# RMS norm statistics by short columns: squares added on VectorE, root and reciprocal on 128x4, spread by four matmuls

## The reference

```python
def rms_norm(t, w):
    tf = t.astype(jnp.float32)
    y = tf * lax.rsqrt(jnp.mean(tf * tf, axis=-1, keepdims=True) + NORM_EPS)
    return (y * w.astype(jnp.float32)).astype(t.dtype)

def modulate(h, shift, scale):
    return h * (1.0 + scale[:, None, :]) + shift[:, None, :]
...
        h = modulate(rms_norm(x, mix_norm[layer]), sh1, sc1)
...
        x = x + g1[:, None, :] * y
        h = modulate(rms_norm(x, ffn_norm[layer]), sh2, sc2)
        x = x + g2[:, None, :] * swiglu(h, ffn_w1[layer], ffn_w2[layer])
```

## Time and profile before

| | us |
|---|---|
| median of three runs | 4071.24 |
| the runs | 4070.95, 4071.24, 4079.08 |
| span of the profiled execution | 4077.1 |
| TensorE busy | 3536.0 |
| VectorE busy | 1910.2 |
| ScalarE busy | 1105.3 |

### The profile page before, as it was taken

One profiled execution on the slowest core, in us unless ns is written; L12 is line 12 of the kernel. 1 busy time (PEld: TensorE's weight loads), 2 busy tenths in 40 slices (PEclk: granted clock), 3 DMA queues, 4 the chain that ended last, 5 costly groups with the idle time before them and its releaser, 6 DMA issues. The chain is left out here.

```text
span 4077.1 us, 35826 instructions
## 1 busy us (share of the span) xinstructions
PE 3536.0 (87%) x12594; PEld 2393.3 (59%) x12594; DVE 1910.2 (47%) x2585; ACT 1105.3 (27%) x1425; POOL 77.1 (2%) x148
## 2 busy tenths in 40 slices
PE   4997889999789998858999963999979679989987
PEld 1444468877458787523888521588847347558433
DVE  5756266536358824243664498366333433143001
ACT  1221243233432214211442101244242322132000
POOL 0000000000000000000000000000000000000000
PEclk9897999999899999868999986999989889999988
DMA  5331146522035532101333210233323112222111
GB/s 211 96 123 53 42 153 192 188 83 73 16 119 196 172 99 79 52 0 52 93 97 96 69 47 11 73 98 95 96 81 100 36 48 86 82 63 97 52 62 62
DMA packets 100408, 360.85 MB, mean 89 GB/s; under 512 B 11152, under 2 KB 11169, under 8 KB 100065
## 3 DMA queue, kind: packets, MB, share of 16 engines
q1 hardware_dynamic: 77936, 276.07, 21.1%
q0 software_dynamic: 20080, 75.27, 5.7%
q10 hardware_dynamic: 2304, 8.39, 0.5%
HBM read 357.59 MB, written 2.10 MB: 88 GB/s over the span
## 5 line engine op out<-in xcount | busy, mean ns | idle before, releaser
L1583 DVE TENSOR_TENSOR weight_lo<-weight_ring,weight_hi 128x1024 fp32r<-128x1024 f32 (+1 forms) x390 | 468.7, 1204 | 931.5 <-ACT weight_hi L1104 927.5
L1104 ACT ACTIVATE weight_hi<-weight_ring 128x1024 fp32r<-128x1024 f32 (+1 forms) x390 | 406.9, 1045 | 1266.0 <-PE proj_banks L683 926.3
L683 PE MATMUL proj_banks<-h_hi,weight_hi 128*128 128x512 f32 x1584 | 617.2, 390 | 9.6 <-DVE weight_lo L1583 9.6
L683 PE MATMUL proj_banks<-h_lo,weight_hi 128*128 128x512 f32 x1584 | 617.0, 389 | 0.0
L683 PE MATMUL proj_banks<-h_hi,weight_lo 128*128 128x512 f32 x1584 | 616.9, 389 | 0.0
L640 PE MATMUL proj_banks<-h_tiles,weight_ring 128*128 128x512 f32 x768 | 348.2, 616 | 62.1 <-DVE scratch L1591 38.3
L1617 DVE RECIPROCAL scratch<-scratch 128x512 f32<-128x512 f32 (+1 forms) x39 | 129.2, 3312 | 479.9 <-ACT scratch L1104 479.9
L683 PEld LDWEIGHTS proj_banks<-h_hi,weight_hi 128*128 128x128 f32 x1584 | 297.8, 188 | 73.5 <-issue 11.6
L683 PEld LDWEIGHTS proj_banks<-h_lo,weight_hi 128*128 128x128 f32 x1584 | 297.6, 188 | 61.9
L683 PEld LDWEIGHTS proj_banks<-h_hi,weight_lo 128*128 128x128 f32 x1584 | 297.8, 188 | 61.5
L640 PE MATMUL proj_banks<-scratch,weight_ring 128*128 128x512 f32 x640 | 294.9, 624 | 27.0 <-DMA weight_ring<-in_w_dnr 27.0
(11 more groups left out here) (256 smaller groups left out, 4277.8 us busy)
## 6 DMA issues: line engine op xcount, KB each, us to landing
weight_ring<-in_w_up SPq DMA_DIRECT2D x176, 512.0 KB, 3.6
ada_ring<-in_ada POOLq DMA_DIRECT2D x96, 512.0 KB, 3.8
weight_ring<-in_w_dn SPq DMA_DIRECT2D x64, 512.0 KB, 3.5
weight_ring<-in_w_br SPq DMA_DIRECT2D x32, 512.0 KB, 3.6
weight_ring<-in_w_upr SPq DMA_DIRECT2D x32, 512.0 KB, 3.5
weight_ring<-in_w_dnr SPq DMA_DIRECT2D x32, 512.0 KB, 4.4
scratch<-in_ada POOLq DMA_DIRECT2D x24, 512.0 KB, 4.6
weight_ring<-in_w_dn SPq DMA_DIRECT2D x32, 384.0 KB, 3.1
```

Source lines behind the costliest of these rows:

```text
L683: last = mm(proj.banks[:, u % RING, :], stationary(split0 + n)[:, w], moving(k), start=k + m == 0, stop=k == kt - 1 and m == 2)
L1104: return nc.scalar.activation(out, in_, func, **kw)
L1583: return v.tensor_tensor(out, a, b, op)
```

## The change

In words, for each of the eleven norms:

- **Sum.** TensorE no longer multiplies eight squared tiles of 512 columns by ones. VectorE adds squares 1 to 6 to square 0 (`sum_up`). TensorE then takes 128 tokens of the total as the stationary operand and one column of ones as the moving one, four times, and again four times with square 7. The sums stand in four columns of PSUM, tokens on partitions.
- **Where the adds stand.** For norms 1 to 8 in the residual loop: ahead of the residual of tile k, from k = 2 on, the square of k-1 is added. For norms 0, 9 and 10 all six stand at the head of VectorE's norm.
- **Root and reciprocal** are taken of 128x4. A root of one constant column is put after square 6.
- **Spread.** Four matmuls, with column j of the reciprocal read as a 128x128 stationary operand (step 0) and the identity as the moving one, write 128x512 to a second bank ("bc", r), and the multiply reads it from PSUM. TensorE waits for the reciprocal there.
- **Weight chunks.** ScalarE's two roundings move from ahead of square 7 to behind it, ahead of the root. VectorE's two splits move from ahead of the reciprocal to behind it, ahead of the wait for the spread.
- **Modulated and split.** ScalarE makes h_hi from H(k) with gain and shift in one pass; H(k) itself is modulated by VectorE, in place, ahead of each subtraction. In plain split norms VectorE now waits for each multiply.
- **dn0 to dn3.** `round_down` is gone; ScalarE rounds the chunks among the squares.

```diff
-    k = [("ss", 0)]
+    k = [("ss", 0), ("bc", 0)]
...
+PLAIN_SPLIT = (4, 5, 7)
+STD, INV = 160, 164
...
     def norm(r):
-        sum_squares(("ss", r), lambda k: (s["sq_ready"], 8 * r + k + 1), lambda k: T(squares_at(r) + k), KD)
+
+        bank = open_bank(mix, ("ss", r))
+        for half, (sem, n) in enumerate(((s["sq_summed"], 6 * (r + 1)), (s["sq_ready"], 8 * (r + 1)))):
+            pe.wait_ge(sem, n)
+            for j in range(NB):
+                squares = T(squares_at(r) + (KD - 1 if half else 0))
+                last = mm(bank[:, j:j + 1], squares[:, j * P:(j + 1) * P], c.square("ones")[:, 0:1], start=half + j == 0, stop=half + j == NB,
+                          skip_group_check=True)
+        last.then_inc(mix.full_sem, 1)
+        bank = open_bank(mix, ("bc", r))
+        pe.wait_ge(s["rstd_ready"], r + 1)
+        for j in range(NB):
+            last = mm(bank[:, j * P:(j + 1) * P], c.small[:, INV + j:INV + j + 1].broadcast_to([P, P]), c.square("ident"), start=True, stop=True)
+        last.then_inc(mix.full_sem, 1)
...
-    def round_down(layer):
-
-        for n in range(SPLIT_RING, 3 * KD):
-            round_chunk(f"dn{layer}", n)
...
             elif r in NORM_AFTER:
-                act.wait_ge(*proj.emptied((NORM_AFTER[r], k)))
+                stage = NORM_AFTER[r]
+                if stage in SPLIT:
+                    for n in range(max(3 * k + 2, SPLIT_RING), min(3 * k + 5, 3 * KD)):
+                        round_chunk(stage, n)
+                act.wait_ge(*proj.emptied((stage, k)))
...
-            if r in SPLIT_UP and k == KD - 2:
-
-                up = SPLIT_UP[r]
-                for n in range(SPLIT_RING):
-                    round_chunk(up, n)
-        root(("ss", r), T(RSTD), D)
+            if k == KD - 2:
+
+                st.link(f(c.small[:, STD:STD + 1], eps, ACT.Sqrt))
+        if r in SPLIT_UP:
+
+            for n in range(SPLIT_RING):
+                round_chunk(SPLIT_UP[r], n)
+        act.wait_ge(*mix.filled(("ss", r)))
+        ins = f(c.small[:, STD:STD + NB], mix.bank(("ss", r))[:, 0:NB], ACT.Sqrt, scale=1.0 / D, bias=eps)
+        ins.then_inc(mix.emptied(("ss", r))[0], 1)
...
-                ins = f(H(k), H(k), ACT.Identity, scale=c.g(use, k), bias=c.m(layer, part, k))
-                ins.then_inc(s["h_raw"] if r in SPLIT_NORMS else s["h_ready"], 1)
                 if r in SPLIT_NORMS:
-                    round_h(r, k)
+                    st.done(f(c.norm_hi(r, k), H(k), ACT.Identity, scale=c.g(use, k), bias=c.m(layer, part, k)), s["h_rounded"])
+                else:
+                    f(H(k), H(k), ACT.Identity, scale=c.g(use, k), bias=c.m(layer, part, k)).then_inc(s["h_ready"], 1)
...
+    def sum_up(r, k):
+
+        total = T(squares_at(r))
+        dve.wait_ge(s["sq_ready"], 8 * r + k + 1)
+        st.done(tt(total, total, T(squares_at(r) + k), ALU.add), s["sq_summed"])
+
     def norm(r):
+        if r not in NORM_AFTER:
+            for k in range(1, KD - 1):
+                sum_up(r, k)
+        dve.wait_ge(*mix.emptied(("ss", r)))
+        st.done(v.reciprocal(small[:, INV:INV + NB], small[:, STD:STD + NB]), s["rstd_ready"])
         if r in SPLIT_UP:
             for n in range(SPLIT_RING):
                 rest_chunk(SPLIT_UP[r], n)
-        inverse(("ss", r), T(RSTD))
+        dve.wait_ge(*mix.filled(("bc", r)))
+        rstd = mix.bank(("bc", r))
...
-                st.done(tt(H(k), X(k), T(RSTD), ALU.mult), s["xn_ready"])
+                ins = tt(H(k), X(k), rstd, ALU.mult)
+                st.done(ins, s["xn_ready"])
...
-                ins = stt(out, X(k), c.v(name, at + k), T(RSTD), ALU.mult, ALU.mult)
+                ins = stt(out, X(k), c.v(name, at + k), rstd, ALU.mult, ALU.mult)
...
+        dve.sem_inc(*mix_release(mix, ("bc", r)))
         if r in SPLIT_NORMS:
             for k in range(KD):
+                if r in MODULATED:
+                    use, layer, part, _ = MODULATED[r]
+                    dve.wait_ge(s["h_rounded"], 8 * SPLIT_NORMS.index(r) + k + 1)
+                    st.link(ts(H(k), H(k), c.g(use, k), ALU.mult, c.m(layer, part, k), ALU.add))
...
     def residual(stage, gate=None, bias=None):
 
+        after = [r for r in NORM_AFTER if NORM_AFTER[r] == stage][0]
         for k in range(KD):
...
+            if k >= 2:
+                sum_up(after, k - 1)
             dve.wait_ge(*proj.filled(key))
```

More of the change, by code:

```diff
@@ L228, in mixing_keys @@
         k += [("av", *units[n - 2])] if n >= 2 else []
-    k += [("ss", 1), ("ss", 2)]
+    k += [("ss", 1), ("bc", 1), ("ss", 2), ("bc", 2)]
     k += [("stat_s", t) for t in range(8)] + [("pool", g) for g in range(4)]
@@ L234, in mixing_keys @@
         k += [("sb", h - 2)] if h >= 2 else []
-    k += [("ss", 3), ("ss", 4)]
+    k += [("ss", 3), ("bc", 3), ("ss", 4), ("bc", 4)]
     k += [("acol", 0)]
@@ L241, in mixing_keys @@
         k += [("mn", h, 0), ("mn", h, 1), ("md", h), ("stat_m", h)]
-    k += [("ss", 5), ("ss", 6), ("lnm", 0), ("lnv", 0), ("ss", 7), ("ss", 8), ("ssc", 0), ("ss", 9)]
+    k += [("ss", 5), ("bc", 5), ("ss", 6), ("bc", 6), ("lnm", 0), ("lnv", 0), ("ss", 7), ("bc", 7), ("ss", 8), ("bc", 8), ("ssc", 0)]
+    k += [("ss", 9), ("bc", 9)]
     k += [("rot_r", t) for t in range(8)]
@@ L247, in mixing_keys @@
     k += [("sgu", t) for t in range(2)]
-    k += [("ssy", 0), ("ss", 10), ("ssy", 1)]
+    k += [("ssy", 0), ("ss", 10), ("bc", 10), ("ssy", 1)]
     return k
@@ L305, in __init__ @@
         self.acc = sb("ada_acc", [P, 8])
-        self.small = sb("small", [P, 160])
+        self.small = sb("small", [P, 168])
         with ExitStack() as mixing:
@@ L330, in __init__ @@
             "x_loaded", "c_loaded", "constants", "setup", "late", "pool_loaded", "dft_loaded", "cond_loaded", "ctx_loaded", "act_chain", "dve_chain",
-            "cond_ready", "pos_ready", "trig_ready", "ada_used", "ada_copied", "ada_first", "mod_ready", "sq_ready", "xn_ready", "h_ready",
+            "sq_summed", "std_ready", "rstd_ready", "cond_ready", "pos_ready", "trig_ready", "ada_used", "ada_copied", "ada_first", "mod_ready", "sq_ready", "xn_ready", "h_ready",
             "iq_ready", "idx_used", "gate_ready", "span_ready", "decay_ready", "gla_ready", "head_normed", "head_roped",
@@ L1117, in round_h @@
     def round_h(r, k):
-        n = 8 * SPLIT_NORMS.index(r) + k + 1
-        act.wait_ge(s["h_raw"], n)
+        act.wait_ge(s["h_raw"], 8 * PLAIN_SPLIT.index(r) + k + 1)
         st.done(f(c.norm_hi(r, k), H(k), ACT.Copy), s["h_rounded"])
@@ L1279, in swiglu @@
                     f(T(52 + p), proj.banks[:, u % RING, :], ACT.Silu).then_inc(proj.empty_sem[u % RING], 1)
-        round_down(layer)
     norm(1)
@@ L1633, in norm @@
                 elif r in SPLIT_NORMS:
-                    ins.then_inc(s["h_raw"], 1)
+                    st.done(ins, s["h_raw"])
                 else:
```

## The result

The changed kernel takes 4096.61 us (median of four runs, 4091.3 to 4103.98) against 4071.97 before, a ratio of 1.0055 with a 95% interval of 1.004 to 1.0071. The forecast was 4038, with a range of 4024 to 4054: it said 33 us faster, and the kernel is 25 us slower. The miss is 58.6 us.

What follows compares the result with a forecast made beforehand. The prediction took TensorE's standstills at eleven RMS norms between projections as the bound. Gains of 15.9, 11.7, 4.6, 7.1, 3.3 and 2.0 less losses of 4.1, 4.5 and 3.0 made 33.0 us saved: 4038, range 4024 to 4054.

Steps and rivals of the forecast that it cites:

- the sum: Adding the gains and losses of the eleven norms and the clock: 33.0 us saved, taken off the median, 4038.
- clock term: TensorE at half clock after norms 2, 3 and 10 too: 3 us lost together, between nothing and 6.
- (d): Rival: step-0 stationary tile loads slowly in the spread's eight passes; at 1 us a pass about 4105; chance 0.03.
- three signs of being wrong: TensorE's small passes longer than 0.25 us, spread ending after the splits, or half clock far into the next stage.
- The front of the norm: From D, TensorE's start on the sum of squares, to the first multiply: D+6.65 instead of D+12.5, 5.9 us earlier.
- 0.177: Price in us of one pass of TensorE's 128x1 sum matmuls, taken from a row of 128x8 passes.
- rival (a): TensorE's small matmuls in the norms cost 0.43 us a pass: 20 to 25 us less saved, 4060; chance 0.11.
- Rival (c): The multiplies' PSUM reads are dearer by a fixed term: 5.7 us less saved, 4044; chance 0.05.
- norms 8 and 9: Norm 8's sum ends earlier, 3.3 us taken; norm 9, partly hidden, 2.0 us taken.
- Norm 0: Six adds in a row, not hidden by residuals: first multiply at 70.4 against 66.38, 4.1 us lost.
- Norm 10: Six adds in a row after the last residual: 4.0 us lost, and 0.5 in the back, 4.5.
- The back of the norm: Modulated split norms after the first multiply: VectorE's 10.4 us of modulation and subtraction ends last, 0.6 us lost.

Runs made afterwards that it cites:

- fifth kernel: The changed kernel with `small` back at 160 columns and the eight new columns in a tile behind all others: 4036.01 us, ratio 0.991.
- first experiment: The kernel before with `small` at 168 columns instead of 160, no instruction changed: 4132.72 us, ratio 1.014.
- twelfth kernel: The changed kernel with `small` at 224 columns instead of 168: 4037.74 us, ratio 0.9909.
- tenth kernel: The fifth kernel with ScalarE instead of VectorE modulating tiles 2 to 7 in the modulated norms: 4023.34 us, ratio 0.988.
- third kernel: The kernel before with `small` at 176 columns instead of 160: 4096.4 us, ratio 1.0056.
- the second: The changed kernel with `small` at 176 columns instead of 168: 4061.15 us, ratio 0.9967.
- ninth kernel: The fifth kernel with TensorE summing all eight squares itself in norms 0, 9 and 10, without VectorE's adds: 4033.76 us, ratio 0.9903.
- eleventh kernel: The fifth kernel with TensorE's direct sums in norms 0, 9 and 10 and ScalarE modulating six of eight tiles: 4028.08 us, ratio 0.9887.

## Why the prediction was wrong

**The step that failed** is the sum. It adds up eleven norms and a clock term, and takes everything else over unchanged. That left out one edit of the diff, `small` from 160 to 168 columns, whose price isn't an instruction: +60 us by the pair of the fifth kernel and the kernel after. None of the rivals held it; (d), the slower one, named 4105 for a slow spread, and the spread took 1.98 us. None of the prediction's three signs of being wrong showed in norm 1 either: all three were inside the norms.

**The front of the norm** was right: first multiply at D+6.52. A 128x1 pass took 0.12 us (0.95 for eight), not 0.177, so rival (a) falls, and so does (d). The row behind the 0.177 had been read without its clock: its passes start every 0.21 us where the granted clock was 0.50 and every 0.11 where it was 1.00. The eight spreading passes end at 514.94, before the two splits are through at 515.21.

**PSUM.** Eight multiplies took 5.73 us where they took 5.78 with both operands in SBUF. Rival (c) falls: the fixed term that the Trainium skill (VectorE: DVE Perf Modes, TRN2 errata) gives for PSUM doesn't show in this form.

**The norms one by one**, as the length of each stage from sum to sum (behind norm 8 the marks are the two sums `ssy` ahead of and behind norm 10). The first measured column is the kernel before less the fifth kernel, both at distance 0. The second is the first experiment less the kernel after, both at 224, so that the passes cancel there too:

| norm | forecast | at distance 0 | at 224 |
|---|---|---|---|
| 1, 2, 3 | 5.3 each | 5.9, 5.2, 5.9 | 6.0, 5.3, 4.6 |
| 4, 7 | 5.9 each | 6.6, 6.2 | 5.4, 6.4 |
| 5 | 4.6 | 4.5 | 4.2 |
| 6 | 7.1 | 6.9 | 9.5 |
| 8 and 9 | 3.3 + 2.0 | 7.0 | 7.4 |
| 0 | -4.1 | -1.2 | 0.2 |
| 10 | -4.5 | -3.4 | -6.9 |

The columns add up to 43.8 and 42.1, and the medians of the same pairs differ by 35.6 and 36.1; the forecast was 33.0. The rest is scatter of single executions. For the first column its place in the runs can be said: a time is some 1.7 us longer than its span in these runs, so the profiled execution of the kernel before lies 7 us above its median and that of the fifth kernel 1 below. (The prediction set a span beside times when it called it 5.9 above the median; nothing hung on that.) The twelfth kernel's stages repeat the first column to 0.1 us, but for norm 0.

Norm 0 was right at its place, though the table doesn't show it. The first multiply moved from 66.38 to 70.73 in the fifth kernel, and the first projection pass from 68.15 to 72.47. What hid the loss lies behind it, in a stretch of small matmuls from 350 to 455 us: it took 103.7 us at a granted clock of 0.69 in the kernel before, 100.8 at 0.73 in the fifth and 105.2 at 0.67 in the twelfth, whose norm 0 comes out at -3.6.

Norm 10 is -5.1 at its place: from the last residual's end to the next stage it was 25.7 us before and is 30.8 in the fifth kernel and in the twelfth. The table's -3.4 and -6.9 have the long feed-forward behind it in them.

**The back of the norm** was right in what ends last. VectorE's row of eight modulations and subtractions starts at 521.02 and is what TensorE waits for; the tenth kernel took six of the eight modulations out of it and won 2.6 us in this norm.

**The clock term** was mis-sized. The half clock that the prediction expected did come: in the fifth kernel the granted clock is 0.50 at 911 to 914 (norm 2) and at 1160 to 1166 (norm 3), some 24 us behind D, where the kernel before had 1.00 and 0.96. But both kernels have another stretch at half clock earlier in the norm, and that one moved forward: in norm 2 from 11.4 to 18.2 us behind D before, and from 3.0 to 13.3 in the fifth, in part while TensorE waits. Over the stretch from D+14 to D+40 (in norm 10 counted from the last residual's end) the mean granted clock is 0.84, 0.92 and 0.86 in norms 1 to 3 of the kernel before, and 0.87, 0.93 and 0.87 in the fifth: no loss left there. Only norm 10 fell, from 0.99 to 0.87. So the 3 us are at most norm 10's, whose whole loss at its place, this included, is 5.1 where 4.5 and a part of the 3 were forecast.

With the tiles in their place the sum would have stood: 4036 against 4038. That is partly luck: norms 8 and 9 gave 2 us more than taken, the clock cost less, and norm 10 cost more. The chance of 0.03 for slower was too low for what the forecast left unpriced, since it came from rivals inside the norm only.

## What to carry to other kernels

A diff that changes the size of one tile moves every tile allocated behind it: list the addresses before and after, and price the operands that moved, above all if thousands of instructions read them. Put new small tiles behind all others, or keep the distance between the two operands of the float32r matmuls; here a multiple of 256 bytes was worth 60 us, more than the 36 us of the whole change to the norms. And compare the mean duration of untouched instructions first: the pace of the 720 passes gave the cause away in one row.

## What the runs showed of the hardware

- **A float32r pass depends on the distance between its operands.** 0.2267 us for 128x512 at the full clock where the starts of weights and activations differ by a multiple of 256 bytes, 0.2289 at 192 more, and 0.2323 to 0.2342 at 32, 64, 96, 128, 160 and 224 more; distances in between were not all of one kind (240 fast, 248 slow). For float32, 64 matmuls took 54.93 us at each of four distances. The Trainium skill (TensorE: Matmul & The Clock Gate, Step-by-step: what each phase is for) says that TensorE reads stream and weights through two independent ports, so that loading the next weights takes no read bandwidth from the running matmul. No row here shows the ports, but the sentence alone doesn't account for these rows: what a pass costs depends on where one operand lies relative to the other.
- At the distance 192 the pace isn't settled by the place alone. The same 720 passes took 165.05 us in the third kernel and 168.89 in the second, whose tiles have the same addresses, and in the second the pace changed between two stages of one execution. Why is open.
- **Small passes are cheap**: 0.12 us for a 128x1 float32 pass with weights of its own at full clock, 0.215 at a granted clock of 0.50 (13.78 for 64, norm 9 of the ninth kernel), and 0.22 (3.54 for 16) in norm 0, where TensorE had done nothing before.
- **The clock isn't the same for the same work.** In the last feed-forward TensorE waits for weights at intervals. Here are the windows of the same part of it in the ninth and in the eleventh kernel:

```profile
3781.00:3811.00 30.00, 26.17 (x62) 11.42 (x61) 0.00 (x0) 1.23 (x2) 0.00 (x0) 1.00 0.18 70
```

```profile
3780.00:3810.00 30.00, 25.95 (x55) 11.05 (x55) 0.00 (x0) 1.23 (x2) 0.00 (x0) 0.89 0.19 70
```

  The same instructions at the same pace of loads, and the granted clock is 1.00 in the one and 0.89 in the other. So a gain of 2 to 4 us can't be read from one pair of executions or from stage lengths alone, as norms 0 and 10 showed; the timeline at the place of the edit shows it.
